# Moving the operands of the three-term matmuls to other SBUF offsets, by spacers of 32 to 256 bytes

## What is computed

```python
for i in range(2):                     # first block
    x = x + (conformer_conv if i == 0 else diff_attention)(rms_norm(x))
    x = x + memory_cross_attention(rms_norm(x), mem)
    x = x + swiglu(rms_norm(x))        # (silu(h @ w_gate) * (h @ w_up)) @ w_down, hidden 2816
x = rms_norm(x)
# second block: three attention branches and a windowed attention, then
h = h + rms_norm(mixed @ w_out)
u = causal_dwconv(rms_norm(h) @ w_up)  # 1024 -> 5632
h = h + rms_norm((gelu(u_gate) * u_up) @ w_down)
```

## The kernel before

| Tensor | Start before | Modulo 1024 | Start with the change | Modulo 1024 |
|---|---|---|---|---|
| raw[0], raw[1] | 0, 8192 | 0 | same | 0 |
| whi[0], whi[1] | 16384, 24576 | 0 | same | 0 |
| wlo[0], wlo[1] | 32768, 40960 | 0 | same | 0 |
| X, SQ | 49152, 57344 | 0 | +32 | 32 |
| Hhi, Hlo | 65536, 73728 | 0 | +32 | 32 |
| H2, MEM, EW | 81920 | 0 | +128 | 128 |
| FH (Ohi, Olo) | 98304 | 0 | +256 | 256 |
| KVr, MKV | 120832 | 0 | +256 | 256 |
| FL, A | 188224 | 832 | 154112 | 512 |
| cst | 153600 | 0 | +23040 | 512 |

## Time and profile before

### The profile page before, as it was taken

One profiled execution on the slowest core, in us unless ns is written; L12 is line 12 of the kernel. 1 busy time (PEld: TensorE's weight loads), 2 busy tenths in 40 slices (PEclk: granted clock), 3 DMA queues, 4 the chain that ended last, 5 costly groups with the idle time before them and its releaser, 6 DMA issues.

```text
span 1218.9 us, 24046 instructions
## 1 busy us (share of the span) xinstructions
PE 1176.6 (97%) x9142; PEld 1120.1 (92%) x9142; DVE 876.5 (72%) x1480; ACT 611.4 (50%) x1072; POOL 63.7 (5%) x53
## 2 busy tenths in 40 slices
PE   9999999999999999998999999999979899999997
PEld 9988898999999999778989999999967589999997
DVE  6999886676665587565767666566896757999954
ACT  6764654544445444344445444455455745656542
POOL 0576000000000000000000000000000000000000
PEclk9999999999999999999999999999988889999999
DMA  7554453455556556214525555555553213545563
GB/s 280 175 199 145 139 173 104 139 174 187 191 173 204 180 184 237 76 44 182 173 70 173 194 185 172 184 200 189 209 195 118 70 36 122 173 172 185 190 208 108
DMA packets 32008, 198.42 MB, mean 163 GB/s; under 512 B 3776, under 2 KB 6080, under 8 KB 9024
## 3 DMA queue, kind: packets, MB, share of 16 engines
q1 hardware_dynamic: 29440, 193.09, 45.9%
q10 hardware_dynamic: 2496, 4.33, 1.1%
HBM read 194.12 MB, written 1.05 MB: 160 GB/s over the span
## 4 chain that ended last, share of the span: by engine, by line
PE 83%; DVE 10%; ACT 3%; issue 2%; DMA 2%; ACTq 0%; DVEq 0%; SPq 0%
PE acc L490 21%; PE acc L492 21%; PE acc L491 21%; PE acc L526 7%; PE acc L506 2%; DVE wlo L1455 2%; PE acc L773 2%; DMA raw<-weights 2%; DVE wlo L1450 1%; PE sc L737 1%; PE tp L490 1%; PE tp L491 1%; PE tp L492 1%; PE st L641 1%; PE tp L762 1%
## 5 line engine op out<-in xcount | busy, mean ns | idle before, releaser
L490 PE MATMUL acc<-Hhi,whi 128*128 128x256 f32 x1368 | 389.4, 285 | 4.0 <-DVE wlo L1455 3.9
L491 PE MATMUL acc<-Hlo,whi 128*128 128x256 f32 x1368 | 387.1, 283 | 0.0
L492 PE MATMUL acc<-Hhi,wlo 128*128 128x256 f32 x1368 | 387.1, 283 | 0.0
L1003 ACT ACTIVATE whi<-raw 128x1024 fp32r<-128x1024 f32 x160 | 169.2, 1058 | 358.1 <-PE acc L492 329.0
L1450 DVE TENSOR_TENSOR wlo<-raw,whi 128x1024 fp32r<-128x1024 f32 (+1 forms) x158 | 193.4, 1224 | 116.8 <-ACT whi L1003 115.4
L490 PEld LDWEIGHTS acc<-Hhi,whi 128*128 128x128 f32 x1368 | 262.5, 192 | 5.3 <-DVE wlo L1455 3.4
L491 PEld LDWEIGHTS acc<-Hlo,whi 128*128 128x128 f32 x1368 | 262.6, 192 | 0.2
L492 PEld LDWEIGHTS acc<-Hhi,wlo 128*128 128x128 f32 x1368 | 262.5, 192 | 0.0
L1455 DVE TENSOR_TENSOR wlo<-raw,whi 128x1024 fp32r<-128x1024 f32 (+1 forms) x158 | 193.3, 1223 | 1.6 <-ACT whi L1006 0.4
L490 PE MATMUL acc<-FH,whi 128*128 128x256 f32 x608 | 173.0, 285 | 4.9 <-DVE FH L2085 3.3
L492 PE MATMUL acc<-FH,wlo 128*128 128x256 f32 x608 | 171.6, 282 | 0.0
(11 more groups left out here) (356 smaller groups left out, 2024.6 us busy)
## 6 DMA issues: line engine op xcount, KB each, us to landing
raw<-weights SPq DMA_DIRECT2D x177, 1024.0 KB, 4.9
MEM<-mem_in SPq DMA_DIRECT2D x2, 1024.0 KB, 7.5
held<-weights SPq DMA_DIRECT2D x2, 1024.0 KB, 6.0
E<-A ACTq DMA_DIRECT2D x12, 128.0 KB, 2.2
X<-x_in ACTq DMA_DIRECT2D x4, 256.0 KB, 5.3
raw<-weights SPq DMA_DIRECT2D x4, 256.0 KB, 6.4
MEM<-consts ACTq DMA_DIRECT2D x2, 512.0 KB, 4.8
out<-MKV SPq DMA_DIRECT2D x4, 256.0 KB, 2.1
```

The costliest lines, as they stand in the source:

```text
L490: pe.matmul(dst, w, x, start=first, stop=False)
L491: pe.matmul(dst, w, xl, start=False, stop=False)
L492: return pe.matmul(dst, wl, x, start=False, stop=last)
L1003: act.activation(whi[j][:, 0:HALF, 0:width], raw[j][:, 0:HALF, 0:width], ACT.Copy).then_inc(hi_out, 1)
```

## The change

Four tensors that nothing uses are allocated, of 8, 24, 32 and 64 floats per partition (32, 96, 128 and 256 bytes), ahead of `X`, `H2`, `FH` and `FL`. `FL` and `A` move from the end of the allocation to just behind `MKV`. No instruction is added, removed or moved.

```diff
         wlo = [sb(f"wlo{j}", [P, KC, MB], F32R) for j in range(2)]
+        sb("apart_x", [P, 8])
         X = sb("X", [P, DC, S])
         SQ = sb("SQ", [P, DC, S])
         with ExitStack() as shared:
             Hhi, Hlo = sb("Hhi", [P, DC, S], F32R, shared), sb("Hlo", [P, DC, S], F32R, shared)
         held = [sb(f"held{j}", [P, KC, MB]) for j in range(2)]
+        sb("apart_h2", [P, 24])
         with ExitStack() as shared:
             H2 = sb("H2", [P, 2, DC, S], F32R, shared)
         H2hi, H2lo = H2[:, 0, :, :], H2[:, 1, :, :]
         MEM = sb("MEM", [P, DC, S])
         EW = sb("EW", [P, 2, 2, 2 * S])
+        sb("apart_fh", [P, 32])
         FH = sb("FH", [P, FC, S], F32R)
         with ExitStack() as shared:
             KVr = sb("KVr", [P, 4 * DC, S], F32R, shared)
         MKV = sb("MKV", [P, 4 * DC, S])
+        sb("apart_fl", [P, 64])
+        with ExitStack() as shared:
+            FL = sb("FL", [P, FC, S], F32R, shared)
+        A = sb("A", [P, FC, S])
         cst = sb("cst", [P, NCONST + DC])
...
         cmask_b = sb("cmask_b", [P, 32], BF16)
-        with ExitStack() as shared:
-            FL = sb("FL", [P, FC, S], F32R, shared)
-        A = sb("A", [P, FC, S])
```

## The result

The changed kernel takes 1209.01 us in the median of 4 runs (1207.49 to 1212.59), the kernel before 1219.73 us beside it (4 runs, 1216.64 to 1221.83). The ratio is 0.9929, with a 95% interval of 0.9909 to 0.9949: **faster by 0.7%**, some 9 us (the two medians alone lie 10.7 us apart). The forecast was 1208.2 us. The profiled execution took 1212.59 us, with a span of 1210.8; it is the slowest of the four, and the two traces differ by 8.1 us only. Lines have moved by 4: L490, L491 and L492 are now L494, L495 and L496.

What follows compares the result with a forecast made beforehand. TensorE was taken to bound the kernel, by number of matmuls times pace. Moving operands off the weights' offset gave -10.8 us, FH and FL -0.9, so 1219.9 - 11.7 = 1208.2 us, range 1204.4 to 1222.5.

Steps and rivals of the forecast that it cites:

- What bounds the kernel: Whole kernel: time is very nearly number of matmuls times their pace; with no instruction changed, only the pace can move.
- Hhi, Hlo and H2: Streams moving off the weights' offset, with those of Ohi and Olo: 4896 matmuls from 120.0 to 117.8 ns, -10.8 us.
- my bound of 117.5: Best pace assumed for the moved streams: 117.5 ns a matmul.
- the cover that I had called thin: up2: VectorE's 108.74 us still fit under TensorE's 114.4; if VectorE set the pace, at most 2.1 us lost.
- The bound from the 30-column loads: The 117.5 ns limit, read from matmuls with only 30 stationary columns, 2.35 us / 20.
- FH and FL, the step that failed: down stages: 422 matmuls at 120.0 ns gain 0.9 us; 1162 at 117.8 unchanged, at worst +2.6 us.
- rival 3: 32 frees Hhi, Hlo and 128 H2, but FH and FL fall back: 9.1 us gained, 2.6 lost, 1213.4 us; chance 0.10.
- My chosen mechanism with 0.40: Operands at the weights' offset modulo 1024 run at 120.0 ns; moved ones take 117.8, giving 1208.2 us; chance 0.40.
- my signs: Expected profile: gu0 at 117.8 ns, weight loads 188 ns, gu0 118.8 us, down0 at one pace around its stall.
- wrong altogether: What would refute the forecast: a gain in plain float32 stretches, or a pace under 117.5 ns.
- which I had counted at nothing: pw1 (384 matmuls) and win (360): no gain, since the wait for wlo hides a faster matmul.
- The rival that placement does not matter: All streams: placement is not the cause, streams stay locked, 1219.9 us within 1 us; chance 0.15.

Runs made afterwards that it cites:

- f_alone: Changed kernel without the spacers ahead of X and H2: FH at 256, FL at 512, the rest at 0; 1220.69 us, ratio 1.0017 to the kernel before.
- fl_far: Changed kernel with FL at 832 instead of 512 modulo 1024, still behind MKV; 1208.53 us, ratio 0.9920 to the kernel before.
- shift_all: Kernel before with everything, weights too, 32 bytes further, so no distance changes; 1217.75 us in a single run.
- h32_alone: Changed kernel with only Hhi and Hlo (with X and SQ) 32 bytes off, all others back modulo 1024; 1208.65 us, ratio 0.9910 to the kernel before.
- all32: Changed kernel with only the 32-byte spacer ahead of X, so Hhi, Hlo, H2, FH, FL at 32; 1206.64 us, ratio 0.9904 to the kernel before.
- all192: Changed kernel with one spacer of 192 bytes ahead of X and no other; 1196.29 us, ratio 0.9806 to the kernel before.
- all448: Changed kernel with one spacer of 448 bytes ahead of X and no other; 1198.98 us, ratio 0.9828 to the kernel before.
- all160: Changed kernel with one spacer of 160 bytes ahead of X and no other; 1206.88 us in a single run.
- d192_64: Changed kernel with other spacers: Hhi, Hlo, FH and FL at 192 modulo 256, H2 at 64; 1198.32 us in a single run.

## Why the prediction was right, point by point

**What bounds the kernel, and that only the pace can change.** Right in the main: 9142 matmuls before and after, and the difference lies in TensorE's stretches. The clock took a part too, in diffo (below).

**Hhi, Hlo and H2.** The forecast had 2.2 ns on 3936 matmuls of Hhi and Hlo, 8.7 us. The profile has 3.1 us in gu0 (121.13 to 118.01 from its first to its last tile), 2.1 in gu1, 1.3 in up2, 0.5 each in memq0, diffk and memq1, 0.3 in diffv and 0.5 in their first tiles: 8.8 us. The sum is right because two errors cancel. gu0 gained 3.3 ns a matmul, a pace under my bound of 117.5. up2's pace of 117.0 ns is worth 2.9 us, but its waits (steps of 140 ns and more, as far as they are longer than the pace) grew from 1.7 to 3.3 us, and 1.3 us are left: the cover that I had called thin, with VectorE busy 109.46 of 115.40 us, took back half: 19 such steps instead of 3, most of them where a tile begins whose wlo VectorE had finished only 130 to 350 ns before. The bound from the 30-column loads was no bound at all: the runs have 113.3. diffq gained 0.3 us, 0.4 were forecast.

**FH and FL, the step that failed.** I wrote that 512 off is as bad as 0 and that FL was going there, and still took no change for the 1162 matmuls at 117.8, and a gain of 0.9 us for the others and of 1.7 for the stages of Ohi and Olo. The profile: memo0 23.21 us before and after, nothing gained; down0 +0.6, down1 +0.6, down2 +1.1, a **loss of 2.3 us**. f_alone confirms it with 1.0017. The forecast was 4.9 us too good in these terms together. The mechanism that happened is rival 3, word for word (32 frees Hhi and Hlo, FH and FL fall back, a pattern of 256 bytes), which had a chance of 0.10 and 1213.4 us. My chosen mechanism with 0.40 was only half right; that its 1208.2 us came out so near is luck. Two of my signs say so too: gu0's 116.7 ns is a pace under 117.5, which I had named as wrong altogether, and down0 has one pace on both sides of its stall, as forecast, but the slow one.

**Why the time came out near it all the same.** pw1 gained 1.2 us and win 0.6, which I had counted at nothing because a wait for wlo hides a faster matmul: their waits took back little of what the matmuls between them saved (nothing in pw1, 0.4 us of 0.9 in win). And diffo is 1.5 us shorter because of the clock, not the pace: in the kernel before, the granted clock is 0.5, the lower level of 1.2 GHz, from 563.30 to 566.71 us, and 17 of diffo's first steps take some 213 ns; in the kernel after it stays at 1.00 there. In both, TensorE had been idle for 3.33 us just before diffo. f_alone, fl_far and shift_all have that stretch at 0.5, h32_alone and all32 have not; fl_far and the kernel after differ only in where FL and A lie, which diffo doesn't read, so it doesn't follow the places of diffo's operands, and what decides it stays open. The forecast had nothing for it. Against that, 1.1 us went in the sparse attention between win and up2, where other engines and a granted clock of 0.91 in the mean (in both kernels) set the time, and about 0.9 elsewhere. -8.8 - 0.3 - 1.8 - 1.5 + 2.3 + 2.0 = -8.1 us, the difference of the spans.

**The rival that placement does not matter** fell. The Trainium skill, "SBUF — State Buffer", section "Who interferes with whom", has TensorE's two read ports independent and never waiting. The runs disagree with what follows from it for the pace: the same stream takes 120.0 ns at a distance of 0 (f_alone) and 113.3 at 192 (all192), with weight loads of 192 and 188 ns at 0 and 32. By that rule shift_all, f_alone and all192 would have taken the same time; the last two differ by some 24 us. The Trainium skill, "TensorE: Matmul & The Clock Gate", section "Back-to-back issue gap", gives a formula for an isolated matmul that makes an estimated 109 ns for 256 columns. No placement reached that in these streams, which load weights for every matmul; the best is 113.3.

**What stays open.** Why one distance has two paces, and what picks one: all192 had 117.8 in gu0 and 113.4 in gu1, all448 the reverse, and in the earlier trace rows the pace changed at a stall. In the traces nearly every change inside a stage falls at a wait of TensorE (down1 of all192: 113.3 before its wait, 117.8 behind it), but not every one: gu0 of all448 goes from 117.8 to 113.3 and gu0 of all160 from 120.0 to 117.3 with no step over 127 ns between. So the wait is not the whole answer. In gu0, gu1, diffq, memo0 and up2 of the kernel before, and in down of f_alone, all at a distance of 0, it is 120.0 on both sides of every wait. It was not tried to steer it. Nor was it tried to give whi and wlo, or Hhi and Hlo, distances of their own, or to place FH for down2 (which wants 64) apart from down0 (which wants 192). That the two reads meet in a bank of the memory fits the runs, but no row shows a bank.

## What to carry to other kernels

When a stretch is bound by back-to-back matmuls, read the step from start to start and compare stages that differ only in their tensors: here the same matmuls, at the same clock, had steps from 113.3 to 120.0 ns, and the operands' places made the difference. Look at the distance between the moving and the stationary operand modulo 256 bytes; here multiples of 256 (what allocation in power-of-two sizes gives) and 96 cost 120.0 ns, 32 gave 116.7 or 117.7, and 192 gave 113.3 or 117.8, in one execution. This was seen with float32 operands in the rounded form (F32R), 128 stationary and 256 moving columns and a weight load for each matmul; other shapes and types were not tried, and the plain float32 matmuls show nothing of it. A spacer moves everything behind it, so write down for each pair of operands where it ends up, and check that no pair lands on a bad distance: here 32 bytes were worth some 11 us (h32_alone) and the spacers of FH and FL took 2 back (f_alone).

## What the runs showed that I had not expected

- The distance acts modulo 256 bytes and with a sign: moving minus stationary of 32 gives 116.7 or 117.7 ns and 224 gives 118.3; 96 gives 120.0 and 160 gives 117.4 to 118.7.
- A distance of 192 gives 113.3 or 117.8 ns, in one execution. 64 shows the same two, mostly the slower.
- Plain float32 matmuls show nothing of this: with 256 moving columns their records start 216 ns apart, at every placement.
- In up2 a faster pace makes TensorE idle longer before a tile: 1.4 us in the kernel before, 2.0 in all192, all448 and d192_64. Just behind it the granted clock was 0.5 for 3.41 us in all192 and all448, where 16 or so steps take 213 ns, some 1.6 us lost in each. In d192_64 it stayed at 1.00 behind the same idle time, so that time alone doesn't decide.
- With the weights' own distances kept, a shift of everything by 32 bytes does nothing (shift_all).
